# Second model's feed-forward: weight the rows before the product, apply the inverse deviation to each product after it

## The reference, cut to what matters

```python
def rmsnorm(x, w):
    y = xf * lax.rsqrt(jnp.mean(xf * xf, axis=-1, keepdims=True) + EPS)
    return (y * w.astype(jnp.float32)).astype(x.dtype)

        h = rmsnorm(x, ffn_norm_w[l])
        u = causal_dwconv(h @ ffn_w_up[l], ffn_conv_w[l], ffn_conv_b[l])    # three taps
        gate, val = jnp.split(u, 2, axis=-1)
        x = x + (jax.nn.silu(gate) * val) @ ffn_w_down[l]
```

## Time and profile before

| | us |
|---|---|
| median of 3 runs | 4296.6 (4293.11 to 4300.32) |
| profiled execution, its time | 4292.65 |
| its span | 4290.4 |
| PE busy | 3877.8 (90%) |
| DVE busy | 2250.6 (52%) |
| ACT busy | 1584.6 (37%) |
| POOL busy | 317.9 (7%) |

### The profile page before, as it was taken

The page is one execution under the profiler, slowest core; times in us unless marked ns, Lnnn a source line. Parts: engine busy times, 40 slices in busy tenths (PEclk is TensorE's granted clock), DMA queues, the critical chain, the costliest instruction groups (busy, mean ns, idle before and its releaser), DMA issues. The chain is left out here.

```text
span 4290.4 us, 53699 instructions
## 1 busy us (share of the span) xinstructions
PE 3877.8 (90%) x19922; PEld 3017.7 (70%) x19922; DVE 2250.6 (52%) x3880; ACT 1584.6 (37%) x2699; POOL 317.9 (7%) x282
## 2 busy tenths in 40 slices
PE   4987988998999888988999899979879998988998
PEld 3865566777788787865666688856568886657886
DVE  6345576854554474355722455355645525565552
ACT  2234571112442353245621344233434424353431
POOL 0000001111000000100000100103010010401001
PEclk8999999999999999999999999989899999989999
DMA  4100004552223243200012233212123322202332
GB/s 172 58 29 16 4 2 167 186 190 76 86 98 102 98 158 128 67 25 19 1 66 88 76 98 98 98 66 67 37 69 98 98 95 82 79 17 82 94 100 80
DMA packets 86728, 350.82 MB, mean 82 GB/s; under 512 B 9520, under 2 KB 9648, under 8 KB 85680
## 3 DMA queue, kind: packets, MB, share of 16 engines
q1 hardware_dynamic: 72752, 298.53, 21.3%
q0 software_dynamic: 13824, 50.34, 3.5%
HBM read 346.73 MB, written 2.10 MB: 81 GB/s over the span
## 5 line engine op out<-in xcount | busy, mean ns | idle before, releaser
L493 DVE TENSOR_TENSOR split_low<-weight_ring,split_high 128x1024 fp32r<-128x1024 f32 (+1 forms) x456 | 606.4, 1330 | 890.0 <-ACT split_high L485 875.2
L485 ACT ACTIVATE split_high<-weight_ring 128x1024 fp32r<-128x1024 f32 (+1 forms) x474 | 525.6, 1111 | 1039.3 <-PE banks L1356 468.8
L1484 PE MATMUL banks<-normed_high,split_high 128*128 128x512 f32 (+1 forms) x1760 | 653.7, 371 | 78.0 <-DVE normed_low L432 37.9
L1484 PE MATMUL banks<-normed_low,split_high 128*128 128x512 f32 (+1 forms) x1760 | 650.5, 370 | 0.0
L1484 PE MATMUL banks<-normed_high,split_low 128*128 128x512 f32 (+1 forms) x1760 | 650.4, 370 | 0.0
L1484 PEld LDWEIGHTS banks<-normed_high,split_high 128*128 128x128 f32 x1760 | 334.3, 190 | 139.7 <-issue 84.1
L1484 PEld LDWEIGHTS banks<-normed_low,split_high 128*128 128x128 f32 x1760 | 334.6, 190 | 55.2
L1484 PEld LDWEIGHTS banks<-normed_high,split_low 128*128 128x128 f32 x1760 | 333.9, 190 | 55.9
L1356 PE MATMUL banks<-hidden_high,split_high 128*128 128x512 f32 (+1 forms) x880 | 324.4, 369 | 8.5 <-DVE split_low L493 8.5
L1356 PE MATMUL banks<-hidden_high,split_low 128*128 128x512 f32 (+1 forms) x880 | 323.7, 368 | 0.0
L1356 PE MATMUL banks<-hidden_low,split_high 128*128 128x512 f32 (+1 forms) x880 | 323.7, 368 | 0.0
(11 more groups left out here) (286 smaller groups left out, 6595.6 us busy)
## 6 DMA issues: line engine op xcount, KB each, us to landing
weight_ring<-in_up SPq DMA_DIRECT2D x220, 512.0 KB, 3.5
weight_ring<-in_down SPq DMA_DIRECT2D x80, 704.0 KB, 4.0
modulation_ring<-in_ada POOLq DMA_DIRECT2D x80, 512.0 KB, 4.6
weight_ring<-in_merge SPq DMA_DIRECT2D x48, 768.0 KB, 4.5
weight_ring<-in_inputs SPq DMA_DIRECT2D x36, 512.0 KB, 3.5
weight_ring<-in_out SPq DMA_DIRECT2D x32, 512.0 KB, 3.6
latents<-in_ada POOLq DMA_DIRECT2D x16, 512.0 KB, 4.7
weight_ring<-in_xbc SPq DMA_DIRECT2D x16, 512.0 KB, 3.6
```

The costliest lines, as they stand in the source:

```text
L485: act.activation(k.splits[0][:, (n0 + panel) % RING, 0:width], k.slot(n0 + panel)[:, 0:width], ACT.Copy).then_inc(k.high_ready.sem, 1)
L493: dve.tensor_tensor(k.splits[1][:, s, 0:width], k.ring[:, s, 0:width], k.splits[0][:, s, 0:width].bitcast(F32), ALU.subtract).then_inc(k.l ...
L1484: last = pe.matmul(sums(r, half), w, x, start=(c + j == 0), stop=(c == KT - 1 and j == 2))
```

## The change

A new function `split_unscaled` takes the place of the norm in these two calls. It works on `x * gain` without the inverse deviation. ACT splits panel 0, rounds the eight tiles `x * gain` straight from the stream (with panel 1 split after the fourth), and only then takes the square root. DVE subtracts panel 0's low part, makes the eight low tiles in one instruction each (with panel 1's low part after the fifth), and only then inverts. POOL has nothing to do. In `ffn_up` DVE multiplies each product, as it leaves PSUM, by the inverse deviation into an SBUF tile `late`, and the centre and outer taps read that tile in place of PSUM. PE's wait for free banks goes by `scaled_ready` instead of `taps_added`, with one more for the bank of the squares.

```diff
+def split_unscaled(k, block, gain, highs, lows, inverse):
+    @block.scalar
+    def _(act):
+        split_high(k, act, first, 0, width, None)
+        for c in range(KT):
+            act.activation(highs[:, c, :], x[:, c, :], ACT.Copy, scale=gain[:, c:c + 1]).then_inc(
+                k.rounded_ready.sem, 1)
+            if c == 3:
+                split_high(k, act, first, 1, width, None)
+        act.activation(inverse, k.psum[:, SQUARES_BANK, 0:LAT], ACT.Sqrt, bias=k.scalars[:, 12:13],
+                       scale=1.0 / D).then_inc(k.deviation_ready.sem, 1)
+    @block.vector
+    def _(dve):
+        split_low(k, dve, first, 0, width, k.high_ready(1))
+        for c in range(KT):
+            dve.wait_ge(*k.rounded_ready(c + 1))
+            dve.scalar_tensor_tensor(lows[:, c, :], x[:, c, :], gain[:, c:c + 1], highs[:, c, :].bitcast(F32),
+                                     ALU.mult, ALU.subtract).then_inc(k.normed_ready.sem, 1)
+            if c == 4:
+                split_low(k, dve, first, 1, width, k.high_ready(2))
+        dve.wait_ge(*k.deviation_ready(1))
+        dve.reciprocal(inverse, inverse).then_inc(k.inverse_ready.sem, 1)
+        dve.wait_ge(*k.inverse_ready(1))
 # ffn_up, PE
-                    if half == 0:
+                    if half == 0 and late is None:
                         pe.wait_ge(*k.taps_added(i * 8 + 4 * (r - 1)))
+                    elif half == 0:
+                        pe.wait_ge(*k.scaled_ready(i * 4 + 2 * (r - 1)))
+                        if r == 1:
+                            pe.wait_ge(*k.deviation_ready(0))
 # ffn_up, ACT
-                act.activation(buffer(r, half), sums(r, half), ACT.Identity, bias=biases[:, at:at + 1],
+                if late is not None:
+                    act.wait_ge(*k.scaled_ready(2 * f + half + 1))
+                act.activation(buffer(r, half), products(r, half), ACT.Identity, bias=biases[:, at:at + 1],
                                scale=weights[:, centre, at:at + 1]).then_inc(k.centre_ready.sem, 1)
 # ffn_up, DVE, tile(f, r, last)
-            if not last:
-                for half in range(2):
+            if late is not None:
+                dve.wait_ge(*k.taps_added(f * 4 - 4))
+            for half in range(2):
+                if not last:
                     split_low(k, dve, n0, half, width, k.high_ready(f * 2 + (half + 3)))
-            else:
-                split_low(k, dve, n0, count, next_width, k.high_ready(count + 1))
+                elif half == 0:
+                    split_low(k, dve, n0, count, next_width, k.high_ready(count + 1))
+                if late is not None:
+                    dve.wait_ge(*k.product_ready(f * 2 + (half + 1)))
+                    dve.tensor_tensor(products(r, half), sums(r, half), late[:, 4, :], ALU.mult).then_inc(
+                        k.scaled_ready.sem, 1)
             dve.wait_ge(*k.centre_ready(f * 2 + 2))
...
-                    s = sums(r, half)
+                    s = products(r, half)
```

More of the change, by code:

```diff
@@ L1434, in add_product, with ffn_up @@
            squares_ready=tiles if squares else 0, squares_added=tiles - 2 if squares else 0)
-def ffn_up(k, block, highs, lows, hidden_highs, hidden_lows, n, weights, biases, causal):
+def split_unscaled(k, block, gain, highs, lows, inverse):
+    first, width = k.next_panel, KT * P
+    x = k.stream[:, :, CTX:T]
+    @block.scalar
[20 more added lines that the diff above has]
+        dve.wait_ge(*k.inverse_ready(1))
+    k.ahead = 2
+    k.ends(rounded_ready=KT, normed_ready=KT, deviation_ready=1, inverse_ready=1)
+def ffn_up(k, block, highs, lows, hidden_highs, hidden_lows, n, weights, biases, causal, late=None):
     nc, count = k.nc, 2 * FF_TILES
@@ L1455, in buffer, with products @@
         return k.probs[:, 2 * r + half, 0:n]
+    def products(r, half):
+        return sums(r, half) if late is None else late[:, 2 * r + half, :]
     @block.sync
@@ L1562, in ffn_up, with feed_forward @@
            taps_added=4 * FF_TILES, gated_ready=FF_TILES, hidden_ready=FF_TILES, shifted_ready=FF_TILES,
-           roped=FF_TILES)
-def feed_forward(k, columns, stream, normalise, conv, scale, causal, squares):
+           roped=FF_TILES, scaled_ready=0 if late is None else 2 * FF_TILES)
+def feed_forward(k, columns, stream, normalise, conv, scale, causal, squares, gain=None):
     a, b = columns
@@ L1575, in feed_forward @@
         with k.nc.Block() as block:
+            late = None if gain is None else scope.sbuf("scaled_products", P, 5, n)
+            if gain is not None:
+                split_unscaled(k, block, gain, highs, lows, late[:, 4, :])
             with ExitStack() as inner:
-                target = Scope(k, inner).sbuf("normed", P, KT, n)
-                normalise(target, [highs[:, c, :] for c in range(KT)], [lows[:, c, :] for c in range(KT)], block)
+                target = None if normalise is None else Scope(k, inner).sbuf("normed", P, KT, n)
+                if normalise is not None:
+                    normalise(target, [highs[:, c, :] for c in range(KT)], [lows[:, c, :] for c in range(KT)], block)
             with ExitStack() as inner:
@@ L1582, in feed_forward @@
                 hidden = [scope.sbuf(f"hidden_{part}", P, FF_TILES, n, dtype=F32R) for part in ("high", "low")]
-                ffn_up(k, block, highs, lows, *hidden, n, *conv, causal)
+                ffn_up(k, block, highs, lows, *hidden, n, *conv, causal, late)
                 add_product(k, *hidden, FF_TILES, 2, [((a, b), (0, n), stream)], scale, squares, block)
@@ L2226, in second_model_layer @@
     conv = k.vec(f"ffn_conv_w{l}").rearrange("p (a b) -> p a b", a=3), k.vec(f"ffn_conv_b{l}")
-    feed_forward(k, LATC, 0, lambda target, highs, lows, block: plain_norm(k, k.vec(f"ffn_norm{l}"), target, (highs, lows), ahead=2,
-                                                                 block=block),
-                 conv, None, causal=True, squares=True)
+    feed_forward(k, LATC, 0, None, conv, None, causal=True, squares=True, gain=k.vec(f"ffn_norm{l}"))
 def store_result(k):
```

## The result

The changed kernel takes 4310.23 us (median of 10 runs, 4301.61 to 4313.99), beside 4296.99 for the kernel before on the same chip (10 runs). The ratio is 1.0026 [1.0017, 1.0036], which is 11.2 us slower (the two medians lie 13.2 apart). Forecast were 5.1 us less and a range of 4279 to 4306. The times of one kernel fall into two groups, 6 to 9 us apart in the mean, and the profiled execution of the kernel before belongs to its shorter group, that of the changed kernel to its longer one. Its profiled execution took 4310.76 us, with a span of 4308.7 against 4290.4 before.

A forecast was written before the change was run, and what follows sets the result against it. PE, busy for 90% of the span, was taken as the bound. A loss of 17.0 us in loop and end less 22.1 gained at the start made -5.1: 4287.5 from the profiled 4292.65, median 4291.5, range 4279 to 4306.

The forecast's parts named there:

- What bounds the kernel: Whole kernel: PE is busy for 90% of the span and sets the steady `ffn_up` tile's pace, 10.88 us.
- Part 1, the start: Start of both feed-forwards: PE starts at about 3175.6 instead of 3186.07; gains 11.4 and 10.7, together 22.1 us.
- Part 2, the ring: `ffn_up` loop: multiplications close a cycle through ACT and DVE, 11.28 us per tile against PE's 10.88; loss 17.0 with the end.
- the step on DVE's register operation: Between centre and first tap in `ffn_up`: a 0.057 us operation behind the wait, no longer hidden, makes it 0.15.
- to the centre 0.72: `ffn_up` loop, multiplication's start to ACT's centre: 0.68 for the multiplication and 0.03 of handing over.
- the centre 0.78: `ffn_up` loop, length of ACT's centre reading SBUF: kept at 0.78 us, since it has two vector operands.
- to `split_high` 0.67: `ffn_up` loop, from the centre's start to ACT's next `split_high`: 0.67 us, ACT's pitch after a centre.
- The end: Last `ffn_up` tile: both multiplications stand ahead of the taps, 12.49 us to the taps against 11.61, 0.9 more.
- Rival D: PE's new gaps lower its clock: once per tile, 4352; or once at the end, 2 per feed-forward; chance 0.04.
- C: `ffn_up` loop: DVE's three new waits each expose a register step, 11.73 us per tile, 4309; chance 0.13.
- B: `ffn_up` loop cheaper: register operation hidden and centre 0.72, or SBUF taps shorter; 4285, or 4276 below 10.88; chance 0.25.
- forecast A: `ffn_up` cycle of 11.2 to 11.4 us takes back four fifths of the start's gain; 4288.5 to 4296; chance 0.55.

The follow-up runs named there:

- e3: Changed kernel with both of ACT's `split_high` of a tile moved ahead of both centres; ratio 0.9966 to the kernel before.
- e1: Changed kernel's start with the loop of the kernel before, products not multiplied by the inverse deviation; ratio 0.9949 to the kernel before.
- e2: Norm and start of the kernel before with the changed kernel's loop, products multiplied by ones; ratio 1.0076 to the kernel before.
- e8: The changed kernel itself run again, nothing altered; ratio 1.0018 to the kernel before (+7.7 us).
- e5: Changed kernel with the centre reading PSUM, unscaled, still after its multiplication; PE's bank wait by the taps again; ratio 1.0006 to the kernel before.
- e4: Changed kernel with the multiplication of half 0 done twice in each tile; ratio 1.0077 to the kernel before.

## Why the prediction was wrong

- **What bounds the kernel:** right. PE set the pace of a tile before, and e3 shows it does again as soon as the ring is open.
- **Part 1, the start:** right within 0.8 us (21.3 by e1, said 22.1). PE starts 3.12 us after the meeting (said 3.2). The clock fell in both feed-forwards, where I counted on it in the second alone: in the first it fell 1.1 us after PE's restart, so the restart did not keep it up.
- **Part 2, the ring:** the mechanism was right, and so was the step on DVE's register operation: centre to first tap is 0.96 (0.93 said). The step that failed is the size of the lap, 11.47 instead of 11.28, and in it the terms "to the centre 0.72", "the centre 0.78" and "to `split_high` 0.67". Both excesses lie around the centres: multiplication to centre takes 0.78 and 0.77, not 0.72 (handing over in 0.10 and not 0.03); the one centre takes 0.03 more up to the taps, the other 0.05 more in its pitch (0.82 and 0.72 from SBUF, not 0.78 and 0.67). That is 0.06 + 0.05 + 0.03 + 0.05 = 0.19; the other links came out within 0.02 and cancel. I took the handing over from taps to Silu, an instruction with one wait. The change gives the centre a second one, and that became a step of ACT's sequencer, of the same family as the register operation that I did price on DVE's side. The trace of before had such a step to read, in front of ACT's `split_high`, which has more than one wait as well (line 484, 3938 to 3953 us, columns as above). From the end of PE's record to the ACT instruction behind such a step it is 0.12 there (199 times, median), without the step 0.04 (424 times). Price of the lap: 19 x 0.19 x 2 = 7.2 us.

```profile
L484 ACTq EVENT_SEMAPHORE  x3: 38/38/38, 3941.1 to 3952.0; - x3
```

- **The end:** the last tile lost 1.23 (said 0.9), tile 0 lost 0.14 (said nothing): 0.9 us in both feed-forwards.
- **The clock at the end:** left out of the sum. Rival D had it as "once, at the end, 2 per feed-forward"; it cost 1.6 in each, 3.3 in all. I had forecast a wait of 2 to 3 us in the same text, and the clock had fallen within 1.3 us of idle in one of two cases; this belonged in the sum with even odds.
- **The sum:** 7.2 + 0.9 + 3.3 = 11.4 of the 11.3 us by which the loss (28.3 by e2) is above 17.0. With the start's 0.8 this puts the changed part at +7.0 instead of -5.1. The ratio stands at +11.2, 4.2 us more, and e8 at +7.7 shows how much of that isn't steady. In the traces a lower clock in unchanged code stands for it, and no step of the prediction spoke of such a thing.
- **The rivals:** C said slower for another reason: waits that expose the register operations. Between `split_low` and the multiplication there is no gap (1.15 from start to start, 1.14 said), so C's mechanism isn't there on DVE. A step of its family stands on ACT's side instead, 0.06 and 0.05 in a lap. C's turning point, a lap above 11.41, is what was crossed. B is refuted: taps from SBUF take 2.97 against 2.96. D's clock within the tiles is refuted: the window over 220 us of the changed loop, below, has a clock of 1.00. So what TensorE: Matmul & The Clock Gate of the Trainium skill tells in A second HAM failure mode did not happen here, with gaps of 0.3 us before the gate panel.

```profile
3215.00:3435.00 220.00, 213.92 (x924) 1.00 0.30 93
```

The range was too narrow upward for a plain reason: forecast A was given 11.2 to 11.4 for the lap, though 22.1 us of gain stood against 38 laps, where 0.1 us in one lap is 3.8 us in the result. A ring of eleven start-to-start terms is not known to 0.1.

VectorE: DVE Perf Modes of the Trainium skill, in its section on the TRN2 errata, puts ScalarE's fixed cost at 224 cycles from SBUF and 172 from PSUM, which at its 1.2 GHz is an estimate of 0.043 us. The trace agrees: 0.82 against 0.78. For VectorE the same table has the sign the other way round, and the taps (2.97 against 2.96) don't follow it. Had I applied the ScalarE line to both centres, the lap would have come out at 11.37 by that estimate; the rest of the way to 11.47 is mostly the handing over.

## What to carry to other kernels

An instruction put between PSUM and its reader costs nothing by its busy time and everything by its place: look what is queued behind the reader on the reader's engine, and if that work feeds the product again, add up the closed lap and compare it with the pace of the bound engine. The cure is then order, not less work: put what does not depend on the new instruction (here the next panels' rounding) in front of the reader. When a lap comes out within a few per cent of the bound, count the waits of each instruction in it: where a change adds a wait to one that already has one, look for a row with two waits and take the handing over from there. And give the range the error of the lap times the number of laps.

## What the runs showed of the hardware

- From the end of a DVE instruction to the ACT instruction that waits for it: 0.03 us, whether DVE read PSUM (taps to Silu before) or SBUF (the same in the changed kernel). Where the wait is a step of ACT's sequencer of its own, because the instruction has another wait already, it is 0.10, of which the step lasts 0.017; so in the changed kernel and in e5.
- An ACT instruction with vector scale and bias on 512 columns: 0.82 us from SBUF (pitch 0.72), 0.78 from PSUM (pitch 0.67 or 0.68).
- PE's clock behind an idle of about the same length, at the end of `ffn_up`: it fell behind 2.26 and 2.24 us (changed kernel, and so in its other two traces and in e2, 2.23 to 2.25) and 2.25 us (e3, second), and stayed at 1.00 behind 2.27 (e3, first), 2.16 and 2.17 (e5) and 2.82 (e4, both). Behind 1.27, 1.62 and 1.64 it stayed there, and at the start it fell during or soon behind an idle of 3.40 in every case. So the length of the idle alone does not decide at 2 to 3 us; a fall there cost 1.4 to 1.6 us.
- An unchanged stretch of attention takes 175 or 179 us by a clock that is at 2.4 or at 1.2 GHz for 14 us in it. By the times of the executions this changes from one execution to the next; the cause is open.
